# A two-layer trunk and a second block on one core: the gated linear attention woven beside projections and softmax attention

## The reference, cut to what matters

```python
u  = (rmsnorm(x, g_mix)  * (1 + sc1)  + sh1)  @ w_in      # latent rows
uc = (rmsnorm(cx, g_mix) * (1 + sc1c) + sh1c) @ w_in      # context rows
p, gq, gk, gv, gg, rf, rb, aq, ak, av = split_in(u)       # widths 256,256,256,256,256,16,16,512,128,128
o_gc, s_f, s_b = gla_bidir(*gla_features(context), s_zero, s_zero)
o_gl, _, _     = gla_bidir(*gla_features(latent), s_f, s_b)
mix = concat([pool_mixer(p), gla_output(o_gl, gg), latent_attention(ql, k_all, v_all)]) @ w_out
x = x + ga1 * mix
x = x + ga2 * squared_relu_mlp(...)
# layer 0 also updates the context rows in the same way; layer 1 does not
```

## Time and profile before

| | us |
|---|---|
| median of 3 timed runs | 2191.46 (2190.93 to 2196.44) |
| time of the profiled execution | 2201.66 |
| its span, first to last instruction | 2199.9 |
| TensorE busy | 1955.3 (89%) |
| VectorE busy | 1037.3 (47%) |
| ScalarE busy | 864.5 (39%) |
| GpSimd busy | 313.1 (14%) |

### The profile page before, as it was taken

One profiled execution on the slowest core, in us unless ns is written; L12 is line 12 of the kernel. 1 busy time (PEld: TensorE's weight loads), 2 busy tenths in 40 slices (PEclk: granted clock), 3 DMA queues, 4 the chain that ended last, 5 costly groups with the idle time before them and its releaser, 6 DMA issues.

```text
span 2199.9 us, 27249 instructions
## 1 busy us (share of the span) xinstructions
PE 1955.3 (89%) x11407; PEld 1668.6 (76%) x11407; DVE 1037.3 (47%) x1565; ACT 864.5 (39%) x1385; POOL 313.1 (14%) x358
## 2 busy tenths in 40 slices
PE   5877977879999998897789977988899999988999
PEld 2755756668888887675688967878789977868997
DVE  2622257253333335436355545764355545565553
ACT  3342265143223234436244534433244434434442
...
PEclk9988987689999999998799988989899999989999
...
GB/s 281 79 164 104 114 98 39 77 58 77 96 102 93 109 81 69 149 139 114 89 132 193 182 153 93 131 84 20 1 170 188 175 190 155 198 21 115 176 187 137
DMA packets 181382, 265.69 MB, mean 121 GB/s; under 512 B 7558, under 2 KB 102474, under 8 KB 181132
## 3 DMA queue, kind: packets, MB, share of 16 engines
...
HBM read 262.89 MB, written 1.05 MB: 120 GB/s over the span
## 4 chain that ended last, share of the span: by engine, by line
PE 74%; DVE 11%; ACT 7%; DMA 3%; issue 3%; POOL 2%; SPq 0%; POOLq 0%; DVEq 0%; ACTq 0%
PE ps L69 71%; PE ps L77 3%; DVE WLO L86 2%; ACT AR L80 2%; DVE AR L86 2%; DMA RAW<-in_w_in_dram 2%; DVE AR L96 2%; DMA RAW<-in_w_mod_dram 1%; ACT WHI L80 1%; POOL XR L86 1%; POOL SM L86 1%; ACT XN L80 1%; ACT L80 1%; DVE TL L86 1%; DVE SM L99 1%
## 5 line engine op out<-in xcount | busy, mean ns | idle before, releaser
L86 DVE TENSOR_TENSOR WLO<-RAW,WHI 128x1024 fp32r<-128x1024 f32 (+1 forms) x402 | 469.4, 1210 | 354.6 <-ACT WHI L80 354.4
L80 ACT ACTIVATE WHI<-RAW 128x1024 fp32r<-128x1024 f32 (+1 forms) x402 | 390.1, 1020 | 331.0 <-PE ps L69 300.5
L69 PE MATMUL ps<-TH,WHI 128*128 128x256 f32 (+1 forms) x1408 | 433.8, 308 | 21.9 <-DVE WLO L86 14.9
L69 PE MATMUL ps<-TL,WHI 128*128 128x256 f32 (+1 forms) x1408 | 431.8, 307 | 0.0
L69 PE MATMUL ps<-TH,WLO 128*128 128x256 f32 (+1 forms) x1408 | 431.3, 306 | 0.0
L69 PEld LDWEIGHTS ps<-TH,WHI 128*128 128x128 f32 x1408 | 275.1, 195 | 34.6 <-issue 19.6
L80 ACT ACTIVATE AR<-ps 128x512 f32<-128x512 f32 (+3 forms) x258 | 122.8, 491 | 434.4 <-PE ps L69 350.0
L69 PEld LDWEIGHTS ps<-TL,WHI 128*128 128x128 f32 x1408 | 275.4, 196 | 10.2
L69 PEld LDWEIGHTS ps<-TH,WLO 128*128 128x128 f32 x1408 | 275.2, 195 | 10.2
L69 PE MATMUL ps<-WHI,TH 128*128 128x512 f32 (+3 forms) x624 | 247.0, 396 | 12.5 <-DVE WLO L86 8.8
L69 PE MATMUL ps<-WLO,TH 128*128 128x512 f32 (+3 forms) x624 | 235.5, 377 | 0.0
...
## 6 DMA issues: line engine op xcount, KB each, us to landing
RAW<-in_w_mod_dram SPq DMA_DIRECT2D x48, 1024.0 KB, 6.9
RAW<-in_ffn_w_in_dram SPq DMA_DIRECT2D x44, 1024.0 KB, 5.1
RAW<-in_w_up_dram SPq DMA_DIRECT2D x32, 1024.0 KB, 5.4
RAW<-in_w_down_dram SPq DMA_DIRECT2D x32, 1024.0 KB, 5.1
RAW<-in_ffn_w_out_dram SPq DMA_DIRECT2D x20, 1024.0 KB, 5.1
RAW<-in_dil_w_in_dram SPq DMA_DIRECT2D x18, 1024.0 KB, 5.1
RAW<-in_gdn_w_in_dram SPq DMA_DIRECT2D x16, 1024.0 KB, 5.7
RAW<-in_w_in_dram SPq DMA_DIRECT2D x12, 1024.0 KB, 5.8
```

The costliest lines, as they stand in the source:

```text
L69: return Made(None if self.eng is None else self.eng.matmul(o, l, r, start=start, stop=stop))
L80: return Made(None if self.eng is None else self.eng.activation(o, i, f, **k))
L86: return Made(None if self.eng is None else self.eng.tensor_tensor(o, a, b, op))
```

## The change

Five things change, all in the mixer parts of the two layers.

1. The linear attention starts during the projections and goes on beside the softmax attention. A new function `mixers` builds each engine's order. The columns are now projected in the order gr, pq, kv, akv, aq. The first steps of the linear attention (`EARLY`) are woven with the remaining steps of pq and kv; 10 and 9 further steps (`LATE`) with akv and aq and 4 modulation chunks; the rest with the attention, the pooling and 8 chunks (4 in layer 1). The attention starts when the projections have ended, in the four banks that these used.
2. Buffers of its own. The context's linear attention lies in XR (whose rows are loaded anew, 2 MB, on GpSimd's queue at the end of layer 0's mixers), the latent one's in PMD and a part of AR. The pooling matrix is no longer resident but comes as a tile in the stream of weights, in each layer. Both sequences share two PSUM banks (`lring`), where each had three. The exponents' buffers of the attention are three where they were four, and the second rope buffer is gone.
3. Heads as pairs of 64-row products. KZ holds the keys once; the two heads of a pair contract over rows 0-63 and 64-127, one instruction after the other, into different banks. The products of the levels (and of `ac`) do the same. `HM` and the masked copies of the keys are gone.
4. Per level ScalarE runs one Exp of 1024 columns where it ran two of 512 and two masked copies; VectorE one subtraction of 512 columns and one multiplication of 1024; GpSimd keeps only its two subtractions, now in layer 1 too.
5. The attention output is turned and split (`ended`) inside the attention, not in a stage behind it.

```diff
-        KM0 = (AR[:, 8704:9216], AR[:, 9216:9728])
-        MAIN = (AR[:, 9728:10240], AR[:, 10240:10752], AR[:, 10752:11776], AR[:, 9728:10752], AR[:, 11776:13824], KM0)
-        SIDE = (W2[0][:, 0:512], W2[0][:, 512:1024], W2[0][:, 1024:2048], W2[0][:, 2048:3072], W2[1][:, 0:2048], KM1)
+        XR0 = XR[:, 0:2048], XR[:, 2048:3072], XR[:, 3072:4096]
+        PM0 = PMD[:, :], AR[:, 11776:12800], AR[:, 12800:13824]
+        GBUF = {(0, 0): XR0, (0, 1): PM0, (1, 0): (XR[:, 0:2048], XR[:, 1024:2048], None), (1, 1): PM0}
...
+                    for v in range(2):
+                        p = slice(64 * v, 64 * v + 64)
+                        pe.matmul(bs[v][:, 0:128 * nk], QT[p, h % 4, 128 * ti:128 * ti + 128], KT[p, 0:128 * nk], True, True).then_inc(
+                            pe_at, ("s", l, step + v))
...
-                for f in range(2):
-                    b = key("a", li, f)
...
+                b = [key("a", li, f) for f in range(2)]
+                for i in range(2):
+                    for a in range(2):
+                        n0 = 256 * i + 128 * a
+                        for f in range(2):
+                            p = slice(64 * f, 64 * f + 64)
+                            m = pe.matmul(b[f][:, n0:n0 + 128], kx[p, a, 128 * i:128 * i + 128], qx[p, a, 128 * i:128 * i + 128], True, True)
+                m.then_inc(did, ("a", l, li))
...
-                act.act(dk, dk, ACT.Exp).then_inc(did, ("ke", l, li))
-                act.act(dq, dq, ACT.Exp).then_inc(did, ("qe", l, li))
...
-                act.act(g.KM[li % 2], dk, ACT.Copy, scale=HM[:, 0:1]).then_inc(did, ("km", l, li))
-                act.act(dk, dk, ACT.Copy, scale=HM[:, 1:2]).then_inc(did, ("k", l, li))
+                    act.wait_ge(G, ("kd", l, li))
+                    act.wait_ge(V, ("qd", l, li))
+                    act.act(e, e, ACT.Exp).then_inc(did, ("e", l, li))
...
+                dve.tt(o, x, r, ALU.subtract).then_inc(did, ("qd", l, li))
...
+                    dve.tt(e, e, g.GQK, ALU.mult).then_inc(did, ("qk", l, li))
...
+        MODS = [(range(4, 8), range(8, 16)), (range(16, 20), range(20, 24))]
+        EARLY = ((2, 2), (1, 2))
+        LATE = ((10, 9), (2, 9))
+        FULL = ((28, 26), (3, 26))
...
+        def mixers(l, project, attention, pooling, gla, mods):
+            p, gs, m = project(l), [gla(l, sq) for sq in range(2)], [mods(x) for x in MODS[l]]
+            advance(p, solo(l))
+            k = keyed(l)
+            weave((part(p, k), k), *[(part(g, n), n) for g, n in zip(gs, EARLY[l])])
+            weave((p, left(l) - k), *[(part(g, n), n) for g, n in zip(gs, LATE[l])], (m[0], 2 * len(MODS[l][0])))
+            yield
+            rest = [(g, n - e - d) for g, n, e, d in zip(gs, FULL[l], EARLY[l], LATE[l]) if n > e + d]
+            weave((attention(l), souls(l)), (pooling(l), 1 + len(SEQS[l])), (m[1], 2 * len(MODS[l][1])), *rest)
+            yield
...
+                lring.set(4, 5)
+                ring.set(6, 7)
+                order = mixers(l, pe_project, pe_attention, pe_pooling, pe_gla, pe_mods)
+                next(order)
+                aring.set(0, 1, 2, 3)
+                oring.set(6)
+                ring.set(7)
+                next(order)
...
+                    pool.wait_ge(pe_gl[0], ("out", 0, 1))
+                    pool.dma(XRt[:, 0:2, :], T["ctx"][0].rearrange("(t p) d -> p t d", p=128)).then_inc(ld_xr, "ctx")
+                    pool.dma(XRt[:, 2:4, :], T["x"][0].rearrange("(t p) d -> p t d", p=128)).then_inc(ld_xr, "rows")
```

338 lines of the change are left out of this document (138 added, 200 removed).

## The result

The changed kernel takes 2179.95 us (median, 2161.59 to 2184.82) against 2195.66 us of the kernel before, measured beside it: a ratio of 0.9905, 95% interval 0.9879 to 0.993. The forecast was 2055 us, range 2015 to 2120. It is faster, as forecast, but by 16 us instead of 136.

A forecast was written before the change was run, and what follows sets the result against it. TensorE was taken as the bound, hardly more than half used in the second stages. Mixer work of 226.6 and 156.2 us at share 0.85 takes 136 us off 2201.7; less 10.2 profile offset, 2055 us timed, range 2015 to 2120.

The forecast's parts named there:

- the share: Merged mixers: TensorE busy time times clock over length, taken as 0.85, giving 266.6 us in layer 0, 183.8 in layer 1.
- The w_in landings: Layer 0's first stage: four waits on w_in tiles, together 35.1 us; part of them kept in the 0.85.
- The clock: Granted TensorE clock in the merged mixers: above 0.9 in both layers, counted within the 0.85.
- The work terms: TensorE work in the mixers at full clock: 226.6 us in layer 0, 156.2 in layer 1, after pair savings and switches.
- first rival: Scores and level products: the two heads of a pair don't overlap, 41.4 us of work stay, 2104 us; chance 0.15.
- The switches: TensorE changes between 128-row and 64-row products: up to 0.17 us each, half taken, 5.4 and 2.7 us.
- The second rival: Second projection part: weights' landings set its pace, 0.77 of full-speed TensorE, 2102 us; chance 0.18.
- The third rival: Merged mixers: level waits carried into dense stages lower the clock, 2301 us, slower by 110; decides from 0.65 downwards; chance 0.05.

The follow-up runs named there:

- e7: Changed kernel with softmax attention back beside the projections, linear attention behind both, unpaired scores, modulation chunks split 4+8 and 2+6: 2144.2 us, 0.9759 of the kernel before.
- e10: Kernel before, with only the modulation chunks moved towards the second stages (4+8 in layer 0, 2+6 in layer 1): 2157.63 us, 0.9835 of the kernel before.
- e3: Changed kernel plus one 128-row, 512-column filler product ahead of each score product, overwritten by it: 2194.47 us, 0.998 of the kernel before.
- e5: Changed kernel plus filler of eight 128-row, 128-column products ahead of each score product, overwritten by it: 2234.66 us, 1.0162 of the kernel before.
- e1: Changed kernel with no two 64-row products running at once (second head's scores left wrong): 2240.62 us, 1.0192 of the kernel before.
- e9: Changed kernel plus two 64-row, 512-column filler products ahead of each pair of score products: 2215.57 us, 1.0098 of the kernel before.
- e6: Changed kernel with all linear attention steps woven into the attention part, none beside the projections: 2181.48 us, 0.9923 of the kernel before.

## Why the prediction was wrong

**The step that failed is the share.** The prediction says: "Share: between 0.77 (a first stage with its w_in waits) and 0.90 to 0.91 (without), I take 0.85." It is 233.1 / 353.1 = 0.66 in layer 0 and 156.1 / 222.7 = 0.70 in layer 1. The merge did not raise it at all: before, by the same marks, it was 0.68 and 0.74. Both ends of my bracket came from stages in which TensorE's time is mostly projection products, and I applied them to a stretch of which more than half has none: behind the last w_in tile stand scores, transposes, level products and chunks. In layer 0 the forecast was 266.6 us and 86.5 are missing. It left 40.0 us for idle time and clock together (266.6 - 226.6); they took 54.3 + 65.7 = 120.0. That is 80.0 of the 86.5, and the other 6.5 are work. Unmerged, with after's split, layer 0 stands at 279.00 x 0.87 / 319.2 = 0.76 (e7), so the merge, at which the share was to rise, is where it fell.

Two parts of the change worked against each other here. The w_in landings on the chain did go, from 35.1 us to 10.4, as the share of 0.85 assumed in part; but e10 has that from moving chunks alone. Beside it the merge cost more than it brought.

**The clock was not a term of its own.** I multiplied it into the share, took for granted that a busy TensorE has a high one, and expected over 0.9 in both layers. It is 0.78 and 0.84. e3, e5 and e1 show that work put into the same part changes it: full-height products raise it from 0.69 to 0.84 and 0.89, with the longest sum of waits at 14.8 us (e3) for 17.8, and e1 lowers it to 0.63 by making TensorE busier with half-height ones. e3 and e9 differ in the height of the filler, at the same busy share, and stand at 0.84 and 0.77 (part of e9's ran beside a score). So busy time does not give the clock, and what kind of products stand in a part has a share in it. That the mix alone makes after's 0.69 is not shown: e6 has the same kinds of products at 0.77, and after's own executions scatter. Which property of the products counts, beside the rows that they use, is open.

**The work terms were right.** Work was forecast at 226.6 and 156.2 us, and is 233.1 and 156.1. The pairs do overlap (first rival wrong): they save 0.78 us a level for the 0.94 taken, and e1 shows them to be worth 60 us of time in this kernel. The switches cost about what was set.

**The second rival** (landings pace the projection part, share 0.77) came near in one place: that part of layer 0 stands at 131.74 x 0.88 / 152.5 = 0.76, with one landing of 10.39 us on the chain. But e6 takes this part to 123.7 us by moving the linear attention's serial steps alone, without a gain in the sum, so the landings are not all of it.

**The third rival** had the right symptom for another reason. It said that the clock falls as in the old second stages, through waits of the levels. The clock did fall, at 83% busy with waits of 2.7 us and less but for one; the kernel is not slower because the idle time shrank at the same time. It was to decide under a share of 0.65 for both layers, and they have 389.2 / 575.8 = 0.68: the kernel was close to slower.

That the forecast had the direction right is in part luck: without the moved chunks, which it did not price (it says that nothing but the order changes), layer 0 would have come to 342.8 + 33.9 = 376.7 us for 363.9 before, if the merge costs the same at 8+4, which no run shows.
